# Two of the three scatters of a long convolution issued by SyncE in place of GpSimd

## The reference

```
def bidir_long_conv(z, h_fwd, h_bwd, bias):
    L = z.shape[1]
    k = jnp.concatenate([h_fwd, jnp.zeros_like(h_fwd[:1]), h_bwd[1:][::-1]], axis=0)
    kf = jnp.fft.rfft(k.astype(jnp.float32), n=2 * L, axis=0)
    zf = jnp.fft.rfft(z.astype(jnp.float32), n=2 * L, axis=1)
    y = jnp.fft.irfft(zf * kf, n=2 * L, axis=1)[:, :L]
    return (y + z.astype(jnp.float32) * bias).astype(z.dtype)

    x1, x2, v = jnp.split(u, 3, axis=-1)
    filt = hyena_filters(L, fw1, fb1, fw2, fb2, fw3, freq)
    z = v
    for n, gate in enumerate((x1, x2)):
        z = gate * bidir_long_conv(z, filt[:, n, 0], filt[:, n, 1], fbias[n])
```

## Time and profile before

| | us |
|---|---|
| median of three runs | 3747.05 |
| the profiled execution | 3743.57 |
| its span (first to last instruction) | 3741.8 |
| PE busy | 3368.0 (90% of the span) |
| DVE, ACT busy | 2181.8, 1316.5 |
| POOL busy | 314.1 (8%), 510 instructions |
| queue q0 (software) | 51936 packets, 131.27 MB, 16.5% of 16 engines |
| queue q1 (hardware) | 132584 packets, 270.68 MB, 22.3% of 16 engines |

### The profile page before, as it was taken

One profiled execution on the slowest core, in us unless ns is written; L12 is line 12 of the kernel. 1 busy time (PEld: TensorE's weight loads), 2 busy tenths in 40 slices (PEclk: granted clock), 3 DMA queues, 4 the chain that ended last, 5 costly groups with the idle time before them and its releaser, 6 DMA issues.

```text
span 3741.8 us, 47892 instructions
## 1 busy us (share of the span) xinstructions
PE 3368.0 (90%) x18246; PEld 2622.9 (70%) x18246; DVE 2181.8 (58%) x3240; ACT 1316.5 (35%) x2215; POOL 314.1 (8%) x510
## 2 busy tenths in 40 slices
PE   3999867887888899999999988999999979999897
PEld 2888534454467778888778866767777758888685
DVE  8998723333334665555476855555555676666676
ACT  2221222332333443333234643333333353333344
POOL 0111123333330000000000110000000000000000
PEclk9999989888888999999999999999999989999999
DMA  6665879878653132222443531000000223332632
GB/s 220 217 202 197 188 105 140 118 115 135 130 172 110 57 124 84 83 83 81 180 152 96 166 113 40 8 7 7 14 24 0 78 102 110 108 104 87 239 99 87
DMA packets 184985, 410.13 MB, mean 110 GB/s; under 512 B 33279, under 2 KB 60223, under 8 KB 183111
## 3 DMA queue, kind: packets, MB, share of 16 engines
q1 hardware_dynamic: 132584, 270.68, 22.3%
q0 software_dynamic: 51936, 131.27, 16.5%
q10 hardware_dynamic: 288, 5.77, 0.4%
HBM read 262.50 MB, written 81.00 MB: 92 GB/s over the span
## 4 chain that ended last, share of the span: by engine, by line
PE 71%; DVE 12%; DMA 11%; ACT 3%; issue 3%; POOL 1%; SPq 0%; DVEq 0%; ACTq 0%
PE ps L618 18%; PE ps L620 18%; PE ps L619 18%; DMA t2w<-w 4%; PE ps L2367 3%; PE ps L2392 3%; DMA t2z<-s 2%; DMA t2k<-s 2%; PE ps L688 1%; PE ps L2240 1%; DVE mx L2758 1%; PE ps L2264 1%; PE ps L2249 1%; PE ps L2427 1%; PE ps L2330 1%
## 5 line engine op out<-in xcount | busy, mean ns | idle before, releaser
L618 PE MATMUL ps<-HB,gsp 128*128 128x512 f32 x1232 | 488.6, 397 | 37.2 <-DVE HB L794 21.9
L619 PE MATMUL ps<-HB,gsp 128*128 128x512 f32 x1232 | 485.2, 394 | 0.0
L620 PE MATMUL ps<-HB,gsp 128*128 128x512 f32 x1232 | 484.1, 393 | 0.0
L1072 DVE TENSOR_TENSOR gsp<-graw,gsp 128x512 fp32r<-128x512 f32 x330 | 226.4, 690 | 262.7 <-ACT gsp L1051 261.9
L1051 ACT ACTIVATE gsp<-graw 128x512 fp32r<-128x512 f32 x330 | 206.7, 628 | 326.9 <-PE ps L620 265.0
L618 PEld LDWEIGHTS ps<-HB,gsp 128*128 128x128 f32 x1232 | 234.5, 190 | 90.1 <-issue 21.4
L618 PE MATMUL ps<-tsp,wdh 128*128 128x512 f32 x616 | 244.1, 396 | 35.3 <-DVE tsp L1329 35.2
L620 PEld LDWEIGHTS ps<-HB,gsp 128*128 128x128 f32 x1232 | 234.3, 190 | 49.8
L619 PEld LDWEIGHTS ps<-HB,gsp 128*128 128x128 f32 x1232 | 234.6, 190 | 46.8 <-issue 1.0
L619 PE MATMUL ps<-tsp,wdh 128*128 128x512 f32 x616 | 242.4, 394 | 0.0
L620 PE MATMUL ps<-tsp,wdh 128*128 128x512 f32 x616 | 242.3, 393 | 0.0
(11 more groups left out here) (263 smaller groups left out, 7717.2 us busy)
## 6 DMA issues: line engine op xcount, KB each, us to landing
graw<-in_w_gu SPq DMA_DIRECT2D x176, 256.0 KB, 2.6
mring<-in_mod_w POOLq DMA_DIRECT2D x78, 512.0 KB, 4.7
hidden_scratch<-R SPq DMA_DIRECT2D x154, 256.0 KB, 2.4
traw<-hidden_scratch SPq DMA_DIRECT2D x154, 256.0 KB, 2.6
t2k<-s POOLq DMA_DIRECT2D x80, 256.0 KB, 10.1
t2z<-s POOLq DMA_DIRECT2D x160, 128.0 KB, 8.8
t2w<-w POOLq DMA_DIRECT2D x160, 128.0 KB, 5.1
wd<-in_w_dx SPq DMA_DIRECT2D x6, 2816.0 KB, 14.2
```

The lines of the kernel that those rows point to most:

```text
L618: pe.matmul(o, wh, xh, start=start, stop=False, skip_group_check=onto)
L619: pe.matmul(o, wh, xl, start=False, stop=False, skip_group_check=onto)
L620: return pe.matmul(o, wl, xh, start=False, stop=stop, skip_group_check=onto)
L1072: dve.tensor_tensor(gsp[U % 3][:, 1, :], graw[:, q, W_SLOT[i], :], gsp[U % 3][:, 0, :].bitcast(F32), ALU.subtract).then_inc(w.lo, 1)
```

## The change

SyncE's walk takes over the waits and the issues of the t2k scatters (K steps) and of the t2z scatters (Z steps), among its own loads. A chunk's filter load now stands just ahead of the last scatter of K(it,1), with those of K(4,0) ahead of its sixth and eighth; the load of zbuf stands behind the scatters of its Z step. GpSimd keeps the t2w scatters of the M steps and issues the loads of mi and mib ahead of its walk, behind the same wait for the input projection. Sizes, slots, semaphores and the other engines stay as they are.

```
@@ SyncE
             sp.wait_ge(s_us[1], 12 * 32)
-            sp.wait_ge(p_in.full, 24 * 6)
-            sp.dma_start(mi[:], a["k_mi"][:, 0]).then_inc(s_ci, 16)
-            sp.dma_start(mib[:], a["k_mi"][:, 1]).then_inc(s_ci, 16)
 
             for kind, it, o, n in WALK:
                 if kind == "K":
-                    if it == NCH and o == 0:
-                        filter_load(NCH + 2)
-                        filter_load(NCH + 3)
-                    if it < NCH and o == 1:
-                        filter_load(it + 2)
+                    for u in range(8):
+                        if it == NCH and o == 0 and u in (5, 7):
+                            filter_load(NCH + 2 + u // 7)
+                        if it < NCH and o == 1 and u == 7:
+                            filter_load(it + 2)
+                        n2, cc, kb = filter_unit(it, o, u)
+                        b = n["B"] + u
+                        sp.wait_ge(s_be, b + 1)
+                        sp.dma_start(by_partition(t2k, it, n2, 0 if it < NCH else 512 * cc, 512), s1[b % 6][:]
+                                     ).then_inc(s_s1o[b % 6], 16)
                 elif kind == "Z":
+                    for u in range(4):
+                        for h in range(2):
+                            b = n["B"] + 2 * u + h
+                            sp.wait_ge(s_be, b + 1)
+                            for m2 in range(2):
+                                n2, at = (2 * u + m2 + 8 * h, 0) if it < NCH else (m2 + 2 * h, CW * u)
+                                sp.dma_start(by_partition(t2z, it, n2, at, CW), s1[b % 6][:, CW * m2:CW * (m2 + 1)]
+                                             ).then_inc(s_s1o[b % 6], 16)
                     if o == 1 and it + 1 < NIT:
                         sp.wait_ge(s_af, A_END["Z", it, 1])
                         sp.dma_start(share(zbuf, it + 1), u_share(it + 1, 2)).then_inc(s_zl, 16)
@@ GpSimd
+            pool.wait_ge(p_in.full, 24 * 6)
+            pool.dma_start(mi[:], a["k_mi"][:, 0]).then_inc(s_ci, 16)
+            pool.dma_start(mib[:], a["k_mi"][:, 1]).then_inc(s_ci, 16)
             for kind, it, o, n in WALK:
-                if kind == "K":
...
-                elif kind == "Z":
...
-                elif kind == "M":
+                if kind == "M":
                     for u in range(8):
                         d = n["d"] + u
                         pool.wait_ge(s_de, d + 1)
```

## The result

Five runs of the changed kernel have a median of 3772.08 us (3762.70 to 3785.03), five of the kernel before on the same chip 3747.05 us (3739.06 to 3752.88). The ratio is 1.007, 95% interval 1.0039 to 1.0100: slower by 25 us, where I forecast 12 to 13 (3759 us, range 3724 to 3794). The profiled execution took 3785.03 us (span 3783.3), the slowest of the five.

The account below looks back on a forecast made before the run. The convolution was taken as bound by how fast scatters land, limited by the few partitions each writes. 3 chunks x 4, plus 1 for filters, plus 1 for Z(3,1), minus 1 for context gave +13 us: 3759 us, range 3724 to 3794.

Parts of the forecast that it names:

- Issuing: Z steps: issuing 16 t2z from SyncE saves at most 3 us, hidden under landings; 0 in main chunks, -1 us in context.
- mi and mib: Loads issued by GpSimd before its walk, needed only some 70 us later: 0, with a bound of 1 us.
- The loads in line: SyncE's queue: zbuf 2.7 us and filters 1 us cost their own time among the scatters, 3.7 us a chunk.
- t2k and t2z in line at 109 GB/s: K(1,0) to K(1,1): 24 pieces at 2.4 us in line, with start and loads 63.4 us, 5.7 more than before.
- t2w's own queue gives back 18 us: M(0,1), M(1,1), M(2,1): t2w never queues behind t2k, which gives back 5.0 + 6.4 + 6.4 = 18 us.
- the z gate: Before M(1,0): remaining t2k and M's t2w overlap (shift 0) or take turns (t2z 8 us late); middle taken, 4 us.
- The gate of M(1,0): TensorE starts M(1,0) when the last t2z lands; forecast about 4 us later, likewise for each next chunk.
- Sum: Whole kernel: 3 chunks x 4, plus 1 for filters, plus 1 for Z(3,1), minus 1 for the context: +13 us.
- Rival 1: Hardware queue as fast as software queue, M steps' 18 us come through whole: 3729; chance 0.33 with its 68 us case.
- Its small branch of 68 us: 8-partition scatters run on the hardware queue as fast as 32-partition ones, no DMA waits: 3679, chance 0.05 at most.
- Rival 2: Gain in M and loss in the t2z cancel within 0.2% (7.5 us): 3747; chance 0.22.
- Rival 3: Short packets and fewer engines bring scatters to 10% below 109 GB/s, 8 us more per chunk: 3788; chance 0.12.

Follow-up runs that it names:

- experiment 3: The kernel before with only the loads of mi and mib moved to GpSimd: 3746.27 us, ratio 1.0004.
- experiment 2: The changed kernel with the loads of zbuf and of the filters issued by GpSimd: 3773.80 us, ratio 1.0086 against the kernel before.

## Why the prediction was right, and where not

The side and the range were right, by the mechanism that was forecast: t2k and t2z became a stream in line at the rate of few partitions. The loss was forecast at half its size. That 3772 still lies inside the forecast's own range (3747 to 3773), at its very end, is in part luck: 3.7 us a chunk, charged for loads that cost about 1, stood in for a part of a rate that was lower than assumed. The terms:

- **Issuing: right.** SyncE issues eight t2k in 12.20 us, GpSimd one every 1.72: both wait for ScalarE's copies, not for issues. Only Z shows it, with "SPq L1868" at 2.4% of the chain.
- **mi and mib: right,** 0 by experiment 3.
- **The loads in line: wrong.** I charged 3.7 us a chunk, in series. They run on engines that the scatters leave free; moved away they give about 1 us of the 53.9 back, and nothing in the kernel's time (experiment 2).
- **t2k and t2z in line at 109 GB/s: right in kind, mis-sized.** The queue makes 99 in K and 103 in Z. I had taken 109 from a stretch in which the software queue works alone; the same K step before ran at 126. From first to last t2k the chunk grew by 8.9 us, where the forecast had the last copies 5 us later, most of it for the loads. The Trainium skill's rule on 8 entries was weighed in the prediction and then given no weight beyond the choice of 109. It should have had more: the software queue with its overlap was faster than that before (119 GB/s over the whole of K(1,0) to K(1,1)), and that is what the move gave up.
- **t2w's own queue gives back 18 us: wrong.** This is the step that failed. First landings did come earlier, as forecast (in M(0,1) the first in 6.3 us and the next five in 8.0, median; the first four in 11.3 before), but the step as a whole took 24.3 us, not 18 to 20, and before it took 22.9: t2w passes the t2k that wait in the queue, and then meets them on the engines. What I had charged to the z gate (the two overlap or take turns) falls on M itself. M(0,0), with nothing ahead of it, has been the measure of an undisturbed M; it was the right measure of the gap, but not of what a queue of its own would close.
- **The gate of M(1,0): mis-sized,** 10.3 us later counted from K(1,0), not 4: 8.9 in K, 0.9 back between the last t2k and the first t2z (26.2 us, before 27.2), and 2.4 from there to M(1,0) (22.2, before 19.8).
- **Sum.** I had 4 us for each of three chunks and 1 for the start. The profiled executions show 11, 13 and 8 more a chunk, and 9.8 more from the first t2k of all to K(1,0) (120.5 us, before 110.7), 2.9 of it ahead of M(0,0) (71.9 us from the first t2k to TensorE's first t2z products, before 69.0) and 6.6 in the clock of B(0,0), below. These add up to their 42; the medians are 25 apart, so each term is somewhat smaller in the usual execution.

Rival 1 (the bypass wins) needed over 115 GB/s for t2k, t2z and the loads together. From 550 to 603 us they make 115 GB/s (6.08 MB), so by its own number it stood on the edge. But the number was set too low: scatters and loads of the same steps had made 142 GB/s before (540 to 584 us). And what it was to gain, a shorter M, did not come at all. Its small branch of 68 us fell with the half share: the hardware queue did not carry 8 partitions as it does 32. Rival 2 (nothing moves) is excluded by an interval that begins at 1.0039. Rival 3 (the hardware queue is slower at this shape) named what was missing: 6 to 9% below 109 GB/s where it had 10. The truth lies midway between the forecast, 3759, and its 3788.

What stays open: why t2k and t2z together on SyncE cost no more than t2z alone, where all three kinds cost twice as much. The waits show that the kind left behind is waited for less, but no run separates how much of that is queue and how much engines. The landing of t2k and t2z on SyncE's queue, which the prediction had at 11 us or more, stands in no view of the changed kernel. Which eight engines carry the packets was not seen either, nor what holds them to 100 GB/s: in the stretch from 550 to 562 us they begin with slices of 177 to 191 GB/s at 5 and 6 tenths, so eight engines can carry more for a moment. That points to the few partitions of the one scatter under way, as the prediction had it, but no run here changed the number of partitions of these scatters.

## What to carry to other kernels

When scatters dominate the chain, look first at the destinations of scatters that follow each other: the same transfers in another order were worth 99 us here, four times what the choice of the queue cost. Before moving DMAs from GpSimd's queue to SyncE's, count the entries of their slowest dimension: with 8, the stream kept to half of the engines and to about 100 GB/s. A queue of its own takes a transfer past others' issues, not past their packets.

## What the runs showed that I had not expected

- What the 8-partition scatters leave of the engines on the hardware queue is free for others: loads beside them cost about 1 us a chunk and nothing in the kernel's time (experiment 2).
- Full engines say little about the rate. The same t2k took 95.6% of the engines for 126 GB/s in one order and 69.5% for 154 in the other.
- The granted clock moves time about between steps. The 64 matmuls of B(0,0) took 7.33 us before, at a granted clock of 0.99 (527 to 535 us), and 13.89 after, at 0.50 (529 to 544 us): near twice as long, as 1.2 GHz makes of 2.4. The stretches around B(0,0), before and after (columns: us, busy time of PE, PEld, DVE, ACT, POOL, granted clock, the DMA engines' share, GB/s):

```profile
506.00:539.00 33.00, 25.67 (x293) 17.17 (x286) 10.68 (x12) 9.03 (x15) 9.21 (x16) 0.90 0.48 89
```

```profile
509.00:549.00 40.00, 32.80 (x276) 23.68 (x266) 9.75 (x12) 8.65 (x13) 8.29 (x15) 0.66 0.42 80
```

That is 6.6 of the 9.8 us by which the start grew, and no DMA. In B(4,0) it is the other way round (12.68 before, 7.36 after). Of the ten such groups five differ by 0.1 us or more: 6.6, 1.9, 0.1, -5.3 and -0.2, 3 us net. TensorE's busy time over the whole walk is 588.0 us and was 581.0, so the clock explains about 7 at most of the 42 us between the two traces. Why the clock was lower in one than in the other, no run here tells.
